# Eight full down-projection quads recomputed with seven half-width products, and the new engine order around them

## The reference

```python
h = _rmsnorm(x, g_ffn[l])
z = _dwconv_centred(h @ w_up[l], conv_w[l], conv_b[l])   # width 3 over tokens
z_gate, z_val = jnp.split(z, [D_FF], axis=-1)            # D_FF = 2816 = 22 tiles of 128
x = x + (jax.nn.silu(z_gate) * z_val) @ w_down[l]        # 2816 -> 1024
```

## Time and profile before

| what | value |
|---|---|
| timed runs, median of 3 | 1104.0 us (1103.97 to 1104.03) |
| profiled execution, span from first to last instruction | 1102.4 us |
| PE busy | 1092.6 us, 99% of the span, 5328 matmuls |
| DVE, ACT, POOL busy | 531.0, 484.7, 464.8 us (48%, 44%, 42%) |
| granted TensorE clock, mean | 0.999 of 2.4 GHz |
| DMA | 108.79 MB, mean 99 GB/s |

### The profile page before, as it was taken

One profiled execution on the slowest core, in us unless ns is written; L12 is line 12 of the kernel. 1 busy time (PEld: TensorE's weight loads), 2 busy tenths in 40 slices (PEclk: granted clock), 3 DMA queues, 4 the chain that ended last, 5 costly groups with the idle time before them and its releaser, 6 DMA issues.

```text
span 1102.4 us, 16315 instructions
## 1 busy us (share of the span) xinstructions
PE 1092.6 (99%) x5328; PEld 905.8 (82%) x5328; DVE 531.0 (48%) x816; ACT 484.7 (44%) x656; POOL 464.8 (42%) x202
## 2 busy tenths in 40 slices
PE   9999999999999999999999999999999999999997
PEld 7788888888888888888878888888888888888886
DVE  5726755655215551255536368456541355314545
ACT  7835444454225441344557344346432454313451
POOL 5334234344534443544634332435444444444450
PEclk9999999999999999999999999999999999999999
DMA  8222223232222222222522212222332322232222
GB/s 301 93 96 78 68 76 105 78 109 100 96 95 94 97 96 95 96 96 97 180 97 81 91 63 74 95 77 96 115 95 76 115 96 95 79 117 91 96 77 78
DMA packets 33607, 108.79 MB, mean 99 GB/s; under 512 B 3984, under 2 KB 6800, under 8 KB 33552
## 3 DMA queue, kind: packets, MB, share of 16 engines
q1 hardware_dynamic: 32848, 107.03, 29.2%
q10 hardware_dynamic: 704, 1.07, 0.3%
HBM read 105.98 MB, written 2.10 MB: 98 GB/s over the span
## 4 chain that ended last, share of the span: by engine, by line
PE 97%; DVE 1%; DMA 1%; ACT 0%; POOL 0%; SPq 0%; issue 0%; DVEq 0%
PE acc L1044 28%; PE acc L1045 28%; PE acc L1046 28%; PE acc L1170 3%; PE acc L1171 3%; PE acc L1172 3%; PE side L1140 1%; PE side L1258 1%; PE side L1242 1%; DMA x<-xT 1%; PE side L1248 1%; PE side L1221 1%; DVE arena L1019 1%; PE side L1201 1%; PE acc L1132 0%; PE acc L1121 0%
## 5 line engine op out<-in xcount | busy, mean ns | idle before, releaser
L339 POOL TENSOR_TENSOR w_lo<-w_raw,w_hi 128x1024 fp32r<-128x1024 f32 x188 | 453.4, 2416 | 600.6 <-ACT w_hi L348 600.6
L1044 PE MATMUL acc<-xg_hi,w_hi 128*128 128x512 f32 x864 | 338.8, 392 | 0.0
L1045 PE MATMUL acc<-xg_lo,w_hi 128*128 128x512 f32 x864 | 336.3, 389 | 0.0
L1046 PE MATMUL acc<-xg_hi,w_lo 128*128 128x512 f32 x864 | 336.2, 389 | 0.0
L348 ACT ACTIVATE w_hi<-w_raw 128x1024 fp32r<-128x1024 f32 x190 | 200.0, 1057 | 255.2 <-PE acc L1046 219.2
L1044 PEld LDWEIGHTS acc<-xg_hi,w_hi 128*128 128x128 f32 x864 | 162.2, 188 | 35.8 <-issue 2.0
L1046 PEld LDWEIGHTS acc<-xg_hi,w_lo 128*128 128x128 f32 x864 | 162.2, 188 | 33.9
L1045 PEld LDWEIGHTS acc<-xg_lo,w_hi 128*128 128x128 f32 x864 | 162.2, 188 | 33.5 <-issue 0.5
L1044 PE MATMUL acc<-feat_hi,w_hi 128*128 128x512 f32 (+1 forms) x492 | 188.9, 384 | 0.0
L1045 PE MATMUL acc<-feat_lo,w_hi 128*128 128x512 f32 (+1 forms) x492 | 188.8, 384 | 0.0
L1046 PE MATMUL acc<-feat_hi,w_lo 128*128 128x512 f32 (+1 forms) x492 | 188.8, 384 | 0.0
(11 more groups left out here) (131 smaller groups left out, 803.2 us busy)
## 6 DMA issues: line engine op xcount, KB each, us to landing
w_raw<-slabs SPq DMA_DIRECT2D x190, 512.0 KB, 3.3
outT<-arena SPq DMA_DIRECT2D x7, 256.0 KB, 2.3
ln_sb<-ln_gb SPq DMA_DIRECT2D x2, 512.0 KB, 7.7
w_raw<-slabs SPq DMA_DIRECT2D x4, 128.0 KB, 4.6
x<-xT ACTq DMA_DIRECT2D x2, 256.0 KB, 4.6
x<-xT SPq DMA_DIRECT2D x2, 256.0 KB, 5.9
x<-xT ACTq DMA_DIRECT2D x1, 512.0 KB, 7.2
w_raw<-slabs SPq DMA_DIRECT2D x2, 256.0 KB, 6.9
```

The source lines that it names most:

```text
L339: pool.tensor_tensor(w_lo[:, w], w_raw[:, w], w_hi[:, w].bitcast(F32), ALU.subtract).then_inc(lo_done, 1)
L1044: pe.matmul(out, wh, ah, start=first, stop=False)
L1045: pe.matmul(out, wh, al, start=False, stop=False)
L1046: return pe.matmul(out, wl, ah, start=False, stop=last)
```

## The change

The down projection of a full part is taken in two quads of four output tiles. In a quad the two 512-token halves are columns, odd and even feature tiles (blocks of K) are rows, and odd and even output tiles are the other side of a 2x2 scheme. Seven products ("units") replace eight: each unit is 4 feature pairs x 2 output tiles x 3 matmuls of 128x256. A quad was 96 matmuls of 128x512 and is 168 of 128x256.

The scheme needs sums of operands. On the feature side, for each pair, with b11, b12 the even tile's halves and b21, b22 the odd tile's: t1 = b12 - b11, t2 = b22 - t1, t3 = t2 - b11, t4 = b21 - t2. DVE makes them; ACT makes their high parts; DVE makes the low part of t1, and POOL in one 128x768 instruction the low parts of t2, t3 and t4 (`t_low`). On the weight side, for each quad, of slabs raw0 to raw3: s1 = raw1 + raw3, s2 = s1 - raw0, s4 = raw2 - s2, and raw1 becomes raw0 - raw1. In the first quad POOL makes s1 and s2 and DVE s4 and the last; in the second quad DVE makes all four. Each of the seven slabs of a quad needs a high part by ACT and a low part by POOL. The weights of the second quad's slabs 1 and 3 are loaded into other buffers.

PE's order is U1 (raw0), U2 (s1), the first half of U4 (raw2), U3 (s2), the rest of U4, U5 (s4), U6 (the new raw1), U7 (raw3), and then U8 to U14 for the second quad, in a new order of slots. DVE adds every unit's bank to two or four places of x. Code around the boundary, cut:

```diff
+            def t_low(m, k):                       # POOL
+                pool.wait_ge(t_hi_done, 2 * (m * KP + k) + 2)
+                pool.tensor_tensor(t_lo[:, t_at], t_raw[:, H:4 * H], t_hi[:, t_at].bitcast(F32),
+                                   ALU.subtract).then_inc(t_low_done, 1)
...
+                pool.wait_ge(hi_sum, 6 * m + 1)
+                low(0, raw(0)).then_inc(lo_sum, 1)
+                t_low(m, KP - 2)
+                pool.wait_ge(raw_loaded[1], 16 * (n // RING) + 16)
+                pool.wait_ge(raw_loaded[3], 16 * (n // RING) + 16)
+                if m:
+                    pool.wait_ge(sum_done, 6 * m)
+                pool.tensor_tensor(sum_s1, raw(1), raw(3), ALU.add).then_inc(sum_done_pool, 1)
+                pool.wait_ge(sum_done_pool, 2 * m + 1)
+                pool.tensor_tensor(sum_s2[:, :], sum_s1, raw(0), ALU.subtract).then_inc(sum_done_pool, 1)
+                pool.wait_ge(hi_sum, 6 * m + 2)
+                low(1, sum_s1).then_inc(lo_sum, 1)
+                pool.wait_ge(hi_done, n + 1)
+                pool.wait_ge(sum_done, 6 * m + 2)
+                low(2, sum_s2[:, :]).then_inc(lo_done, 1)
+                pool.wait_ge(hi_sum, 6 * m + 3)
+                low(3, raw(2)).then_inc(lo_sum, 1)
+                t_low(m, KP - 1)
+                pool.wait_ge(hi_done, n + 2)
+                low(0, raw(1)).then_inc(lo_done, 1)
+                pool.wait_ge(hi_done, n + 3)
+                low(1, sum_s4).then_inc(lo_done, 1)
...
+                def up_pair(slab, tile, stage, even, odd, t_of, down=None):   # ACT, last pair of a part
...
+                        act.wait_ge(sum_done_pool, 2 * m + 2)
+                        unit_hi(2, sum_s2[:, :], hi_done)
+                    silu(1)
...
+                        act.wait_ge(acc_ready, L * NS + slab + RING)
+                        raw_at(2, first)
+                        unit_hi(3, raw(2), hi_sum)
+                        centre(1, 1)
+                        act.wait_ge(unit_done, 14 * m + 1)
+                        act.wait_ge(sum_done, 6 * m + 2)
+                        unit_hi(0, raw(1), hi_done)
+                    act.wait_ge(t_done, stage * 2 + 2)
+                    on_its_own(act)
+                    act.activation(odd, gated[1], ACT.Copy).then_inc(feat_hi_done, 1)
+                    act.activation(t_of, t_raw[:, H:4 * H], ACT.Copy).then_inc(t_hi_done, 1)
...
+                    gate(0)                        # DVE, up_pair
+                    if k == KP - 1:
+                        dve.wait_ge(sum_done_pool, 2 * m + 2)
+                        dve.wait_ge(raw_loaded[2], 16 * (L * (NS // RING)) + 4 * first + 16)
+                        dve.tensor_tensor(sum_s4, raw(2), sum_s2[:, :], ALU.subtract).then_inc(sum_done, 1)
+                    scale(2)
+                    dve.wait_ge(feat_hi_done, L * NF + part * KT + (KT + 2 * k + 1))
+                    dve.tensor_tensor(lo(0, H), gated[0][:, 0:H], hi(0, H).bitcast(F32),
+                                      ALU.subtract).then_inc(feat_ready, 1)
+                    dve.wait_ge(even_copied, stage + 1)
+                    if k:
+                        dve.wait_ge(t_low_done, stage)
+                    dve.tensor_tensor(t1, gated[0][:, H:S], even_copy, ALU.subtract).then_inc(t_done, 1)
+                    taps(1, 0)
+                    dve.wait_ge(t_hi_done, stage * 2 + 1)
+                    dve.tensor_tensor(lo(H, H), t1, hi(H, H).bitcast(F32), ALU.subtract).then_inc(t_ready, 1)
+                    scale(3)
+                    if k == KP - 1:
+                        dve.tensor_tensor(raw(1), raw(0), raw(1), ALU.subtract).then_inc(sum_done, 1)
+                    taps(1, 1)
+                    gate(1)
+                    dve.wait_ge(gated_done, f + 2)
+                    dve.tensor_tensor(t2, gated[1][:, H:S], t1, ALU.subtract).then_inc(t2_done, 1)
+                    dve.wait_ge(t2_done, stage + 1)
+                    dve.tensor_tensor(t4, gated[1][:, 0:H], t2, ALU.subtract)
+                    dve.tensor_tensor(t3, t2, gated[0][:, 0:H], ALU.subtract).then_inc(t_done, 1)
...
+                    add_unit(0, 0, 0, 0, units + 1, unit_added)      # DVE, down_quads
+                    odd_low(part, KP - 1)
+                    add_unit(0, 1, 1, 1, units + 2, unit_added)
...
+                    dve.tensor_tensor(sum_s1, second_raw[1], second_raw[3], ALU.add).then_inc(sum_done, 1)
+                    add_unit(0, 0, 1, 0, units + 3, unit_added)
+                    dve.wait_ge(raw_loaded[0], loads)
+                    dve.tensor_tensor(second_raw[1], raw(0), second_raw[1], ALU.subtract).then_inc(sum_done, 1)
...
+                def unit(bank, slot_of, pairs, moving, first):       # PE
+                    for k in pairs:
+                        for r in range(2):
...
+                            pe.matmul(out, w_hi[:, a:a + P], xh, start=(first and k == 0 and r == 0), stop=False,
+                                      skip_group_check=True)
+                            pe.matmul(out, w_hi[:, a:a + P], xl, start=False, stop=False, skip_group_check=True)
+                            last = pe.matmul(out, w_lo[:, a:a + P], xh, start=False, stop=(k == KP - 1),
+                                             skip_group_check=True)
...
+                    pe.wait_ge(feat_ready, feats + KT - 1)
+                    unit(0, 0, every_pair, b11, True).then_inc(unit_done, 1)
...
+                    unit(1, 1, every_pair, t1, True).then_inc(unit_done, 1)
+                    pe.wait_ge(lo_sum, 6 * m + 3)
+                    pe.wait_ge(y_ready, ys + 3)
+                    unit(2, 3, range(0, 2), b21, True)
...
+                    unit(0, 2, range(3, 4), t2, False).then_inc(unit_done, 1)
+                    pe.wait_ge(feat_ready, feats + KT)
+                    unit(2, 3, range(2, 4), b21, False).then_inc(unit_done, 1)
+                    pe.wait_ge(lo_done, n + 3)
+                    pe.wait_ge(unit_added, 6 * m + 2)
+                    unit(1, 1, every_pair, b22, False).then_inc(unit_done, 1)
```

More of the change, by code:

```diff
@@ L52 @@
 HALVES = (slice(0, S // 2), slice(S // 2, S))
+H = S // 2
+KP = KT // 2
+QUADS = KT // RING
 TAIL = (KT - 2, KT - 1)
@@ L243, in on_its_own, with raw, raw_of, quads_at @@
             eng.sem_inc(waits_passed, 1)
+        def raw(j):
+            return w_raw[:, j * SLAB:(j + 1) * SLAB]
+        def raw_of(g, j):
+            return second_raw[j] if g and j in second_raw else raw(j)
+        def quads_at(L, part):
+            return L * FULL_PARTS + part, part * PART + (N_FFN + 2 * KT)
         def load_x(eng, g):
@@ L334, in _, with low_slabs @@
                                    ALU.subtract).then_inc(lo_done, 1)
[L335 to L340, removed]
+            def low_slabs(L, first, end):
+                with pool.Fori(L * (NS // RING) + first // RING, L * (NS // RING) + end // RING) as q:
+                    for j in range(RING):
+                        pool.wait_ge(hi_done, q * RING + (j + 1))
+                        low(j, raw(j)).then_inc(lo_done, 1)
@@ L343, in _ @@
+            for L in range(DEPTH):
+                before = RING if L == 0 else 0
+                for part in range(FULL_PARTS):
+                    low_slabs(L, before, N_FFN + part * PART + RING)
+                    low_quads(L, part)
+                    before = N_FFN + (part + 1) * PART
+                low_slabs(L, before, NS)
         @block.scalar
@@ L611, in up_quad, with raw_at @@
                         act.activation(feat(b), gated[b], ACT.Copy).then_inc(feat_hi_done, 1)
[L613 to L619, removed]
+                def raw_at(j, slab):
+                    act.wait_ge(raw_loaded[j], 16 * (L * (NS // RING)) + 4 * slab + 16)
@@ L966, in _ @@
+                with dve.Fori(0, FULL_PARTS) as part:
+                    for k in range(KP):
+                        up_pair(part, k)
+                    down_quads(part)
                 for q in range(LAST_TILES // 2):
@@ L1355, in _ @@
                     if part < FULL_PARTS:
-                        with pe.Fori(0, KT // RING) as q:
-                            for j in (1, 2, 3):
-                                down_tile(j, q, *places)
+                        down_quads(part)
                     else:
@@ L1428, in token_major, with quad_major @@
         return w[2 * s * P:2 * (s + 1) * P, col:col + S].reshape(2, P, S).transpose(1, 0, 2).reshape(P, SLAB)
+    def quad_major(w, rows, m):
+        v = w[rows.start:rows.stop, m * P:(m + RING) * P].reshape(KP, 2, P, 2, 2, P)
+        return [v[:, odd, :, :, i].transpose(1, 2, 0, 3).reshape(P, SLAB) for odd in range(2) for i in range(2)]
     A_W = B_W = 512
@@ L1447 @@
             rows = range(tiles.start * P, tiles.stop * P)
-            slabs += [channel_major(w_down[l], rows, m * P) for m in range(KT)]
+            if len(tiles) == KT:
+                for m in range(0, KT, RING):
+                    slabs += quad_major(w_down[l], rows, m)
```

(2 more changed lines are left out.)

327 lines of the change are left out of this document (307 added, 20 removed).

## The result

| | before | after |
|---|---|---|
| median of the timed runs | 1104.01 us | 1122.05 us (1121.71 to 1124.93) |
| span of the profiled execution | 1102.4 us | 1120.1 us |
| mean granted clock | 0.999 | 0.991 |

The ratio is 1.0169, 95% interval 1.0155 to 1.0183: slower. The forecast was 1124, in the range 1107 to 1134.

What follows compares the result with a forecast made beforehand. PE, busy 99%, was taken as the bound. Per part, 3.2 us saved against stalls gave +6.0 or +3.8, middle 4.9; four parts, 19.6, took the span from 1102.4 to 1122, median 1.6 above: 1124 us, range 1107 to 1134.

Steps and rivals of the forecast that it cites:

- The removal: Inside the quads: 168 matmuls at 0.120 us replace 96 at 0.2267, saving 1.60 us per quad, 3.2 per part.
- steps 1 to 3: Boundary up to U4: s4 waits for s2 and the port, delaying U1 and raw1; PE stands 3.5 us before U4.
- The two orders at s4: When s2 ends, POOL's next low or DVE's s4 takes the port: +6.0 or +3.8 us per part; middle 4.9 taken.
- the upper order: At s4, POOL's next low takes the port first: 9.2 us of stalls against 3.2 saved, +6.0 us per part.
- step 4: Before U5: t_low, DVE's second-quad sums on the port, low U6 and low U5 make PE wait 3.8 us.
- The clock: Behind PE's holes: clock stays at 1.00, as it did over 4 us after the last matmul; no cost.
- the stalls bring down the clock: Rival, chance 0.12 with longer stalls: holes drop the clock to 1.2 GHz, 2.9 us more each; 1136 to 1147 us.
- step 5: After U5: each low part is done before PE asks, tightest at U10 with 0.6 us; no wait.
- The remaining edits: Next part's first waits, slot order, unrolled loops and fewer ACT table loads: costed at nothing.
- The chain is tight: Rival, chance 0.11: nothing late ahead of raw1, no port contention; stalls 2.1 us, -0.9 per part, 1100 us.
- The port costs little: Rival, chance 0.14: s4 runs beside POOL, U1 on time, U4 and U5 wait 2.7 and 1.7; 1109.5 us.
- The scheme does not save: Rival, no chance of its own: 128x256 matmuls run slower than 0.1295 us amid other traffic.

Runs made afterwards that it cites:

- the best order: Changed kernel with POOL's and DVE's queues both reordered at the boundary and the low parts of t2 to t4 back on DVE: 1091.12 us.
- s1 and s2 first: Changed kernel with only t_low of the pair before, s1 and s2 moved ahead of low U1 in POOL's queue: 1115.76 us.
- the dummies before U4: Changed kernel with 24 matmuls of 128x128, in no result, added on PE between U2 and U4: 1121.72 us.
- six-sums kernel: Changed kernel with all six DVE weight sums per part taking their second operand from PSUM instead of SBUF, giving wrong values by design: 1109.86 us.
- s4 alone: Changed kernel with only the first quad's s4 taking its second operand from PSUM instead of SBUF, giving a wrong value by design: 1113.99 us.
- t_low on DVE: Changed kernel with the low parts of t2, t3 and t4 made by DVE again instead of POOL: 1109.54 us.
- s4 late: Changed kernel with the first quad's s4 on DVE moved from before tile 2's scale to behind t3: 1111.28 us.
- DVE's order alone: Changed kernel with DVE's queue reordered (s4 behind tile 3's scale, raw1 earlier, second-quad sums behind additions), POOL's unchanged: 1117.93 us.

## Why the prediction was right, and where it was right by luck

**The removal**: right. 0.120 us inside a unit, and the best order keeps all but 0.8 of the 12.8 us.

**The boundary to U4 (steps 1 to 3)**: right to a few tenths. Zero was at 255.1 us of this trace. raw1 was put at 27.8 and ended at 28.0 (281.85 + 1.21); PE's start of U4 at 32.8 and came at 32.9 (287.96), a wait of 3.54 against 3.5. U1 was 1.1 us late and not 1.7, because the last up matmul came 0.36 later than I had it and the low part 0.24 earlier. The two kernels that move s4 or shorten it show that this is the cause.

**The two orders at s4**: the choice failed. I took the middle of +6.0 and +3.8 per part. POOL's next low part had the port in all four parts (s4 is recorded at 3.17 us each time: it starts 0.31 after low U2, waits for its end, then runs), so the upper order holds, and by my own steps that is +6.0: 1128.

**The wait for U5 (step 4)**: the term that was mis-sized. 3.8 us were forecast, 0 to 1.26 measured. Two things took it down. DVE's second-quad raw1 stands behind the addition that waits for U3's end (L1278 at 293.85), and came at 294.45, too late to hold the port between low U6, which ended at 293.97, and low U5; so low U5 ended at 296.29 and not 297.4. And U4 and U3 ran 1.36 to 2.65 us longer at the lower clock, so PE asked later. The two hang together: 1.36 us earlier, raw1 would have asked at 293.1, in time for the port. Where U3 was not late (s1 and s2 first) that did happen, and low U5 took 3.3 us as step 4 had it. Wait and clock together are 2.38 to 2.65 us a part.

**The clock**: the step failed. I argued from the earlier trace rows that a hole of under 4 us leaves it at 1.00. It fell to 0.50 behind each of the 3.5 us holes. The earlier trace rows show the end of the program, with nothing after it to slow; it was no evidence on a restart. The time survived this because U5 waited for POOL anyway, as the dummies before U4 and the third part of the six-sums kernel show. That is luck: the term was put at nothing for a wrong reason. Where no such wait follows, the same fall made U5 1.6 to 2.3 us longer (s1 and s2 first), and the rival "the stalls bring down the clock" has its mechanism there, at less than its price of 2.9.

**After U5 (step 5)**: nearly right. U10 was called the tightest, with 0.6 to spare; it waited 0.3.

**The remaining edits**, put at nothing: the program outside the four parts came out about 1.1 us shorter, by which edit stays open.

So per part +6.0 by the order that held, less 1.3 for U5 and the clock together, less 0.6 for U1, plus 0.15 at U4 and 0.45 from U10 and the restarts: +4.7, beside a forecast of +4.9. Four parts make 18.8, less 1.1 outside them: 17.7, the difference of the spans. The mechanism of the waits was right; that the size came out so closely is luck, from one term too low (the middle order) and others too high (U5, U1), and from a fall of the clock that a wait hid.

**The rivals.** "The chain is tight" needs s4 off DVE's path; alone that gave 1111, and the tight chain needed POOL's order too. "The port costs little", 1109.5, is nearly what the six sums without the port measured (1109.86), and it was false of the change. "The scheme does not save" is refuted by 1091.12.

## What to carry to other kernels

When two in-order engines feed each other, write out both queues in time around each hand-over and ask what stands behind each wait: here the same work lost 31.6 us in one order and 2.2 in another (0.8 with one step moved to the other engine), and the engines' busy shares (under 60%) showed neither. A hole in PE's work costs more than its length where the clock falls and no later wait takes up the slow matmuls; so sum PE's waits and the slow run behind each together, and look whether the next weight would have been late anyway. Moving a step to the engine with the lowest share is free only if it does not land ahead of something urgent in that engine's queue.

## What the runs showed of the hardware that was not expected

- The granted clock fell from 1.00 to 0.50 behind a hole in PE's work in all four parts at 3.54 us and at 3.2 to 3.5 us, at 2.96 to 2.99 us in seven of eight (six sums, s4 alone), at 3.13 in three of four (t_low on DVE), at 2.33 in three of four (s4 late), and, in the profiled executions, in none of four at 2.41 (DVE's order alone) nor at any of 1.71 or less. The other three executions of the kernel with 2.41 had a lower mean clock (0.995 and 0.996 against 0.999), so the same hole does not always end alike. So between 2.3 and 3.2 us the hole's length alone did not decide; what else does stays open.
- When a POOL instruction's end released a waiting DVE instruction with two SBUF inputs while POOL had its next one queued and ready, POOL had the port every time (3.17 us, four of four; the same with t_low on DVE). A DVE instruction that already waited for the port when POOL's ended had it (2.42 us, and POOL's next took 3.38 and not 2.40).
